# Dilated attention with a lent transposition bank and scores in two lots, in a two-block fp32 kernel with changed order in six other places

## Chip, cores and metric

The kernel runs on one core of one Trainium2 chip. The metric is the device time of the whole program in microseconds (us), lower is better. All matrix products are made from fp32 values that are split in two parts.

## What is computed

x is 256 tokens by 1024, mem and mem_2 are 256 by 1024. First an embedding norm and two layers with a hybrid mixer, attention to a memory, and a feed-forward net, each followed by a norm of the sum; then one layer of a second kind. Cut to what matters here:

```python
x = layer_norm(x)
for l in range(2):
    qa, ka, va, qb, kb, vb, gb, gc, hc, gates = split(x @ w_in[l])
    ya = rms_norm(diff_attention(qa, ka, va))          # 4 heads of two softmax maps (8 maps)
    yb = neighbourhood_attention(qb, kb, vb, rpb[l])   # 8 heads; scores + bias table, masked
    yc = gb * dwconv(gc * hc)                          # 512 channels, 3 taps
    h = sum(sigmoid(gate) * (y @ w_branch)) @ w_mix_out
    x = layer_norm(alpha * x + h)
    h = attention(x @ xa_q, mem @ xa_k, mem @ xa_v) @ xa_o    # 4 heads of 256
    x = layer_norm(alpha * x + h)
    x = layer_norm(alpha * x + conv_ffn(x))
y_mla = mla(rms_norm(x) @ w)                           # 8 heads, causal
y_dil = mixture of 3 groups x 4 heads of dilated attention, softmax over groups too
y_mem = 4 heads of attention to rms_norm(mem_2)
x = x + rms_norm((gated sum of three branches) @ w_o); x = x + rms_norm(conv_ffn(...))
```

## The kernel before

**Weights.** All weights come as one stream in the order of use: 525 halves of 512 KB, each four tiles of 256 columns. SyncE's queue loads them into five slots (RAW = 5; half h waits for the low part of half h - 5). ScalarE writes each half's high part (`weights_hi`, L1076) into one of four split slots (SPLIT = 4; it waits for the last use of half h - 4), VectorE subtracts for the low part (`weights_lo`, L1453). Both do this where `reach(key)` stands in their order: `AT` notes, while TensorE's program is written, at which half each step of TensorE stands, and `reach` splits all halves up to some ahead of that. TensorE waits for the low part of a half before its first tile (`half_at`).

**TensorE.** `linear` multiplies a block: per tile of 128 rows six matmuls (high x high, low x high, high x low, on two halves of 128) into one of four PSUM banks `general` (`ps`), taken in turn by `open_bank`, which waits until the bank's former content is read. Further PSUM: two score banks (`sc`), one for transposed probabilities (`tp`, the trace's probs_transposed; `bank=4` lends it), one for attention outputs (`po`). A transposition is a matmul with the identity (`transposes`, L656; `turn`, L733). Activations are kept as high and low parts too (`xT_hi`, `xT_lo`, `memT_hi`, `memT_lo`, `merged`, `memory_out`, `ffn_act`), in one large area in SBUF, of which the tables of position bias (`bias_tab`) also use a part.

**Attention.** Every set (da 8 maps, na 8 heads, xa 4, mla 8, dil 4, mem 4) is run in steps. At step s TensorE issues the scores of head s, the fillers of that step (blocks of projections that are wanted later), the values product of head s - 2 and the transpositions of head s - 1 (`turn`). In dil a head has three groups, hence three scores, three transposition sets and three copies. ScalarE per step: `exps` (L1119), evacuation of the fillers (L1087), the output of head s - 2, then `probs_out`, the copies of transposed probabilities out of `tp` (L1143). VectorE per step: `normed` of head s - 1 (L1627 to L1641), `maxima` of head s (bias added at L1607, maximum L1616, its negative L1621), then fillers, output and an extra piece of work, if there is one. For dil `exps` needs the negative maximum over all three groups.
Extra pieces of VectorE in da: `gated_conv` chunk 0 at step 4, mask for heads 0 to 3 at step 5 (`masked`, L1714), chunks 1 and 2 at step 6, mask for heads 4 to 7 at 7, chunk 3 at 8. Layer 0 and layer 1 use the same order.

**Beginning.** TensorE: idle work, 16 transpositions of memory, key blocks 0 and 1 of the memory, transpositions of the normed x, key blocks 2 and 3, layer 0. ScalarE: four copies of memT, split to half 4, norm, evacuations. VectorE: the low parts of memT, low parts of two halves, statistics of x, and so on. SyncE's queue: constants, memory, halves 0 and 1, x, halves 2 to 4, the constants' second part, and on.

**GpSimd.** It issues DMAs: rows and columns of parameters, two saves of the transposed memory to DRAM, 32 transfers that build the bias tables in DRAM (L2040, 16 for each layer), then, once the first x is normed and all these have landed, the transfer of a layer's tables into SBUF (L2048).

**Other places.** Behind cross attention four output blocks (`xo`); in layer 1 all eight transposition pairs of the second memory (`mem2T`) stand between blocks 1 and 2. Behind mla stand key block dk 4, the last values of mla, dk 5 and then dil; the last values of dil stand inside the first step of mem.

## Time and profile before

| | us |
|---|---|
| median of three timed runs | 1708.31 |
| lowest and highest | 1705.27, 1708.36 |
| profiled execution, its own time | 1707.84 |
| its span in the trace | 1705.7 |
| TensorE busy | 1647.5 (97%) |
| VectorE busy | 1159.2 (68%) |
| ScalarE busy | 875.8 (51%) |

The trace gives each instruction's start and length from the span's start. Layer 0 begins on TensorE at 48.0, layer 1 near 603, the last layer near 1150; the dilated set runs from about 1323 to 1412, the last feed-forward net from 1514. "[2.54 <-DVE ...]" behind an instruction is the time its engine stood idle ahead of it, and what ended that. The granted clock is a share of full speed, 2.4 GHz; 0.5 is 1.2 GHz.

### The profile page before, as it was taken

What the parts mean: (1) busy time and instruction counts of PE and PEld (TensorE: products, weight loads), DVE (VectorE), ACT (ScalarE), POOL (GpSimd) and SP (SyncE); (2) the same over time, 40 slices, a digit from 0 to 9 for tenths busy, and PEclk for the clock granted to TensorE, in tenths of its full rate; (3) what the DMA queues carried; (4) which work ended last, traced back from release to release, by engine and by line L of the source; (5) the groups of instructions that cost most, each with busy time, mean ns of one, the idle gap of its engine ahead of it and who ended that gap; (6) DMA issues with size and microseconds to landing.
All of it is one profiled execution on the core that took longest, in us unless ns stands there. A gap on an engine that the chain in (4) does not pass through costs nothing.

```text
span 1705.7 us, 32288 instructions
## 1 busy us (share of the span) xinstructions
PE 1647.5 (97%) x13694; PEld 1603.9 (94%) x13694; DVE 1159.2 (68%) x1718; ACT 875.8 (51%) x1317; POOL 39.2 (2%) x59
## 2 busy tenths in 40 slices
PE   7999999999999999999999999998999899999997
PEld 7998999989999999899998999998899789999997
DVE  5568778747666767877874866676566545867776
ACT  4444653545444554465355554446655445465555
POOL 3300000000000000000000000000000000000000
PEclk8999999999999999999999999999999999999999
DMA  9854466535555474446653556564535243545562
GB/s 327 244 194 144 139 208 237 196 112 198 192 179 203 158 248 151 145 140 209 235 216 104 181 180 208 180 199 137 198 124 187 100 163 134 183 151 186 185 209 89
DMA packets 82511, 305.90 MB, mean 179 GB/s; under 512 B 10657, under 2 KB 10785, under 8 KB 80193
## 3 DMA queue, kind: packets, MB, share of 16 engines
q1 hardware_dynamic: 76720, 279.44, 48.7%
q0 software_dynamic: 5648, 24.41, 4.7%
q8 instruction: 108, 1.77, 0.4%
q14 instruction: 35, 0.28, 0.1%
HBM read 300.59 MB, written 6.29 MB: 180 GB/s over the span
## 4 chain that ended last, share of the span: by engine, by line
PE 82%; DVE 12%; ACT 3%; issue 2%; DMA 1%; SPq 0%; DVEq 0%; ACTq 0%
PE general L596 52%; PE general L600 13%; PE scores L638 5%; DVE weights_lo L1453 3%; PE attention_out L638 2%; PE probs_transposed L638 2%; PE scores L714 2%; ACT weights_hi L1076 2%; PE attention_out L774 1%; PE probs_transposed L733 1%; DMA raw_weights<-in_stream 1%; ACT exp_ring L1119 1%; PE attention_out L816 1%; PE probs_transposed L600 1%; DVE softmax_stats L1616 1%
## 5 line engine op out<-in xcount | busy, mean ns | idle before, releaser
L1453 DVE TENSOR_TENSOR weights_lo<-raw_weights,weights_hi 128x1024 fp32r<-128x1024 f32 x525 | 632.7, 1222 | 421.4 <-ACT weights_hi L1076 419.9
L1076 ACT ACTIVATE weights_hi<-raw_weights 128x1024 fp32r<-128x1024 f32 x525 | 552.6, 1057 | 402.5 <-PE general L596 224.6
L596 PE MATMUL general<-xT_hi_part,weights_hi 128*128 128x256 f32 x2432 | 682.7, 281 | 4.4 <-DVE weights_lo L1453 1.9
L596 PE MATMUL general<-xT_lo_part,weights_hi 128*128 128x256 f32 x2432 | 675.0, 278 | 0.0
L596 PE MATMUL general<-xT_hi_part,weights_lo 128*128 128x256 f32 x2432 | 674.9, 278 | 0.0
L596 PEld LDWEIGHTS general<-xT_hi_part,weights_hi 128*128 128x128 f32 x2432 | 459.0, 189 | 12.6 <-issue 7.4
L596 PEld LDWEIGHTS general<-xT_lo_part,weights_hi 128*128 128x128 f32 x2432 | 457.9, 188 | 0.5
L596 PEld LDWEIGHTS general<-xT_hi_part,weights_lo 128*128 128x128 f32 x2432 | 457.7, 188 | 0.0
L1775 DVE SCALAR_TENSOR_TENSOR exp_ring<-general,param_cols,exp_ring 128x255 f32<-128x255 f32 (+1 forms) x176 | 76.8, 478 | 46.4 <-ACT exp_ring L1242 44.9
L1242 ACT ACTIVATE exp_ring<-general,param_cols 128x256 f32<-128x256 f32 x88 | 44.9, 561 | 69.8 <-PE general L596 69.8
L1119 ACT ACTIVATE exp_ring<-exp_ring,softmax_stats 128x256 f32<-128x256 f32 (+3 forms) x56 | 29.3, 525 | 96.9 <-DVE softmax_stats L1621 96.9
L600 PE MATMUL general<-weights_hi,xT_hi_part 128*128 128x256 f32 x272 | 77.7, 286 | 0.9 <-DVE xT_lo_part L1463 0.9
L600 PE MATMUL general<-weights_lo,xT_hi_part 128*128 128x256 f32 x272 | 76.2, 280 | 0.0
L600 PE MATMUL general<-weights_hi,xT_lo_part 128*128 128x256 f32 x272 | 76.2, 280 | 0.0
L638 PE MATMUL scores<-weights_hi,ffn_act_hi 128*128 128x256 f32 x264 | 74.1, 281 | 0.8 <-DVE weights_lo L1453 0.8
L638 PE MATMUL scores<-weights_lo,ffn_act_hi 128*128 128x256 f32 x264 | 74.2, 281 | 0.0
L638 PE MATMUL scores<-weights_hi,ffn_act_lo 128*128 128x256 f32 x264 | 74.1, 281 | 0.0
L1087 ACT ACTIVATE attention_area<-general 128x512 f32<-128x512 f32 x60 | 35.6, 593 | 57.1 <-PE general L596 36.9
L1119 ACT ACTIVATE exp_ring<-scores,softmax_stats 128x256 f32<-128x256 f32 x56 | 26.0, 470 | 66.2 <-DVE softmax_stats L1621 66.2
L600 PE MATMUL general<-weights_hi,merged_lo 128*128 128x256 f32 x192 | 54.0, 281 | 0.0
L600 PE MATMUL general<-weights_lo,merged_hi 128*128 128x256 f32 x192 | 54.0, 281 | 0.0
L600 PE MATMUL general<-weights_hi,merged_hi 128*128 128x256 f32 x192 | 53.9, 281 | 0.0
(293 smaller groups left out, 2994.1 us busy)
## 6 DMA issues: line engine op xcount, KB each, us to landing
raw_weights<-in_stream SPq DMA_DIRECT2D x525, 512.0 KB, 4.2
attention_area<-in_ln_rows POOLq DMA_DIRECT2D x9, 1024.0 KB, 5.0
bias_scratch<-in_rpb POOLq DMA_DIRECT2D x32, 96.0 KB, 14.4
attention_area<-bias_scratch POOLq DMA_DIRECT2D x2, 1536.0 KB, 7.8
memT_hi<-memT_scratch POOLq DMA_DIRECT2D x2, 1024.0 KB, 5.8
memT_lo<-memT_scratch POOLq DMA_DIRECT2D x2, 1024.0 KB, 9.1
attention_area<-in_mem SPq DMA_DIRECT2D x1, 1024.0 KB, 5.0
z_tok<-in_x SPq DMA_DIRECT2D x1, 1024.0 KB, 8.7
```

The lines of the kernel that those rows point to most:

```text
L596: ins = nc.tensor.matmul(ps[b][0:m, half * T:half * T + T], w[wk][:, half * m:half * m + m], x[xk_], start=first, stop=last, skip_group_ch ...
L600: ins = nc.tensor.matmul(ps[b][:, half * T:half * T + T], x[wk][:, half * P:half * P + P], w[xk_], start=first, stop=last, skip_group_chec ...
L638: ins = nc.tensor.matmul(down[2 * t + c][:, q * TILE_N:q * TILE_N + TILE_N], act[xk_][:, kc, t * P:t * P + P], w[wk][:, at:at + TILE_N], s ...
L714: ins = nc.tensor.matmul(dst[:, lo:hi], q, k, start=(c == 0), stop=(c == len(pairs) - 1))
L733: ins = nc.tensor.transpose(tp[:, kt * T + t * P:kt * T + t * P + P], e[:, kt * P:kt * P + P], ident)
L774: ins = nc.tensor.matmul(po[r0:r0 + m, c * T + lo:c * T + T], v, p[:, lo:T], start=first, stop=(g == parts - 1 and kt == 1))
L1076: nc.scalar.activation(hi_half(h), raw_half(h), ACT.Copy).then_inc(*hi_done.more())
L1087: nc.scalar.activation(dst, src[:, :].rearrange("p (c w) -> p c w", w=T), func, **kw).then_inc(*read(key))
L1119: ins = nc.scalar.activation(e, src, ACT.Exp, bias=st("nm", j, t, t + 1), scale=scale if from_psum else 1.0, accum_out=st("sum", j, t, t + 1))
L1242: ins = nc.scalar.activation(cbuf(i % 2, k)[:, c * T:c * T + T], src[:, c * T:c * T + T], ACT.Identity, bias=colp(b, ch, packed), scale=co ...
L1453: nc.vector.tensor_tensor(lo_half(h), raw_half(h), hi_half(h).bitcast(F32), ALU.subtract).then_inc(*lo_done.more())
L1775: ins = nc.vector.scalar_tensor_tensor(d, s, colp(w, 3 * ch + tap, packed), d, ALU.mult, ALU.add)
```

## The change

- Dilated set: the middle group's transpositions go to `ps[3]`, which `open_bank` leaves out as long as it is lent, so that two transposition sets can stand side by side (`turned`, `back`). Scores of groups 0 and 1 stay ahead of the fillers, those of group 2 go behind them; head 0's first two go ahead of block dk 5. The last values of dil go ahead of the memory scores.
- VectorE's extra pieces in da: mask for heads 0 and 1 at step 1, 2 to 5 at step 2, 6 and 7 at step 3; convolution chunks at steps 4, 5, 6 and 8.
- Beginning: the table of ScalarE is loaded ahead of the constants, the first half is split behind the first copy on both engines, three key blocks stand ahead of x's transpositions and the fourth behind them, in bank 4. The constants' second part is issued behind half 10. GpSimd's row and column transfers start with half 3's high part, its 32 bias transfers with half 11's, and the saves of memory come behind the first 16.
- Cross attention: block xq 1 ahead of the set, xq 2 before xv 2, in the stream too.
- Second memory: its transpositions in two lots, behind output blocks 1 and 2.
- Merged, memory output, feed-forward activations and rows move by 32 columns (SHIFT) in the area.

```diff
-        fa_hi, fa_lo = (sb(f"ffn_act_{k}", 4 * T, "area", c, F32R) for k, c in (("hi", 0), ("lo", 4 * T)))
-        mg_hi, mg_lo = (sb(f"merged_{k}", 8 * T, "area", c + 128, F32R) for k, c in (("hi", 8 * T), ("lo", 16 * T)))
-        xo_hi, xo_lo = (sb(f"memory_out_{k}", 8 * T, "area", c, F32R) for k, c in (("hi", 24 * T), ("lo", 32 * T)))
+        fa_hi, fa_lo = (sb(f"ffn_act_{k}", 4 * T, "area", c + SHIFT, F32R) for k, c in (("hi", 0), ("lo", 4 * T)))
+        mg_hi, mg_lo = (sb(f"merged_{k}", 8 * T, "area", c + 128 + SHIFT, F32R) for k, c in (("hi", 8 * T), ("lo", 16 * T)))
+        xo_hi, xo_lo = (sb(f"memory_out_{k}", 8 * T, "area", c + SHIFT, F32R) for k, c in (("hi", 24 * T), ("lo", 32 * T)))
...
-        xa_fillers = [[("xq", 1), ("xv", 2)], [("xq", 2)], [("xq", 3)], [("xv", 3)], [], []]
+        xa_fillers = [[("xq", 2)], [("xv", 2)], [("xq", 3)], [("xv", 3)], [], []]
...
+        def turned(name, g):
+            return ps[3] if name == "dil" and g == 1 else tp
...
+                    if state["lent"] and state["bank"] % 4 == 3:
+                        state["bank"] += 1
...
-                    if n > 0:
-                        pe.wait_ge(*pT_ready.at(n - 1))
+                    back = 1 if name != "dil" or g == 0 else 2 if g == 2 else 3
+                    if n >= back:
+                        pe.wait_ge(*pT_ready.at(n - back))
...
-                    if step < len(js) and name not in ("da", "na"):
+                    if step < len(js) and name == "dil":
+                        if step:
+                            scores(js[step], (0, 1))
+                    elif step < len(js) and name not in ("da", "na"):
                         scores(js[step])
...
                     for key in fillers[step]:
                         filler(key)
+                    if step < len(js) and name == "dil":
+                        scores(js[step], (2,))
...
             linear(("xk", 0), MT, DC, True, before=as_ready("memT"))
-            linear(("xk", 1), MT, DC, True)
+            for i in (1, 2):
+                linear(("xk", i), MT, DC, True)
...
             to_feature("xT0", z3)
-            for i in (2, 3):
-                linear(("xk", i), MT, DC, True)
+            linear(("xk", 3), MT, DC, True, bank=4)
...
+                filler(("xq", 1))
...
-                linear(("xo", 1), XO, DC, False)
-                if l == 1:
-                    for tile in (mem2_tile0, mem2_tile1):
-                        pe.wait_ge(*tile.at(0))
-                    to_feature("mem2T", mem2)
-                for cb in (2, 3):
+                for cb in range(1, 4):
                     linear(("xo", cb), XO, DC, False)
+                    if l == 1 and cb < 3:
+                        for tile in (mem2_tile0, mem2_tile1):
+                            pe.wait_ge(*tile.at(0))
+                        for i in (2 * cb - 2, 2 * cb - 1):
+                            transposes(("mem2T", i), mem2, 2 * i)
...
+            for key in blocks("dq", 0, 4) + blocks("dk", 0, 4):
+                pe.wait_ge(*when_read(key))
+            scores(set_jobs("dil")[0], (0, 1))
             filler(("dk", 5))
-            for key in blocks("dq", 0, 6) + blocks("dk", 0, 6):
+            for key in blocks("dq", 4, 6) + blocks("dk", 4, 6):
                 pe.wait_ge(*when_read(key))
+            if state["uses"][3]:
+                pe.wait_ge(*free[3].at(state["uses"][3] - 1))
+            state["lent"] = True
             held = attention("dil", dil_fillers)
...
-            held = attention("mem", mem_fillers, held=held)
+            held()
+            state["lent"] = False
+            held = attention("mem", mem_fillers)
...
-            act.wait_ge(*const_in.at(0))
+            act.wait_ge(*idle_work_set.at(0))
+            nc.scalar.activation(gain_tmp[:, 3, 0:1], blank[:, 0:1], ACT.Sqrt)
             for i in range(DC // 2):
...
                                      ACT.Copy).then_inc(*mem_hi.more())
+                if i == 0:
+                    split_to(1)
+            act.wait_ge(*const_in.at(0))
             split_to(SPLIT)
...
-                attention("da", da_fillers, {4: lambda: gated_conv((0,)), 5: lambda: masked(0),
-                                             6: lambda: gated_conv((1, 2)), 7: lambda: masked(4),
-                                             8: lambda: gated_conv((3,))})
+                attention("da", da_fillers, {1: lambda: masked(0, 2), 2: lambda: masked(2, 4), 3: lambda: masked(6, 2),
+                                             4: lambda: gated_conv((0,)), 5: lambda: gated_conv((1,)),
+                                             6: lambda: gated_conv((2,)), 8: lambda: gated_conv((3,))})
...
-            pool.wait_ge(*xin.at(0))
+            pool.wait_ge(*hi_done.at(SPLIT - 1))
             load_rows(0)
             pool.dma_start(col[:, :], a["cols"][0]).then_inc(*cols_in.more())
-            pool.wait_ge(*when_read(("memT", DC // 2 - 1)))
-            for k in range(2):
-                part, copy = mem_parts(k)
-                pool.dma_start(copy, part).then_inc(*mt_saved.more())
-            pool.wait_ge(*hi_done.at(SPLIT - 1))
+            pool.wait_ge(*hi_done.at(3 * SPLIT - 1))
...
+                if l == 0:
+                    pool.wait_ge(*when_read(("memT", DC // 2 - 1)))
+                    for k in range(2):
+                        part, copy = mem_parts(k)
+                        pool.dma_start(copy, part).then_inc(*mt_saved.more())
...
-            sp.dma_start(const[:, CONST_FIRST:CONST_N], a["const"][:, CONST_FIRST:CONST_N]).then_inc(*tables_in.more())
             for h in range(RAW, HALVES):
                 sp.wait_ge(*lo_done.at(h - RAW))
                 load_half(h)
+                if h == 2 * RAW:
+                    sp.dma_start(const[:, CONST_FIRST:CONST_N],
+                                 a["const"][:, CONST_FIRST:CONST_N]).then_inc(*tables_in.more())
```

## Rows read from the trace of the kernel before

**Rows 1.** The page: busy time of each engine; the chain that ended last.

```profile
PE 1647.5 (97%) x13694; PEld 1603.9 (94%) x13694; DVE 1159.2 (68%) x1718; ACT 875.8 (51%) x1317; POOL 39.2 (2%) x59
...
PE 82%; DVE 12%; ACT 3%; issue 2%; DMA 1%; SPq 0%; DVEq 0%; ACTq 0%
```

**Rows 2.** Waits of TensorE: what for, us in total, times, longest.

```profile
PE probs_transposed L733 <- ACT probsT_ring L1143: 6.2, 8, 1.7
PE probs_transposed L733 <- DVE exp_ring L1641: 5.1, 2, 2.5
PE scores L714 <- DVE exp_ring L1607: 3.9, 2, 2.6
```

**Rows 3.** Timeline of TensorE, beginning: start, us, what, [idle before].

```profile
6.34 1.94 PE L656 MATMUL general<-constants,attention_area 128*128 128x128 f32 x16 [0.15 <-DMA attention_area<-in_mem]
12.75 0.55 PE L596 MATMUL general<-memT_hi,weights_hi 128*128 128x256 f32 x1 [4.48 <-DVE weights_lo L1453]
...
34.75 0.58 PE L596 MATMUL general<-memT_hi,weights_hi 128*128 128x256 f32 x1 [4.68 <-DVE xT_lo_part L1463]
...
48.00 0.28 PE L596 MATMUL general<-xT_hi_part,weights_hi 128*128 128x256 f32 x1
```

**Rows 4.** Stretches: us, TensorE busy (instructions), granted clock, DMA share, GB/s.

```profile
12.50:19.50 7.00, 6.75 (x36) 0.58 1.04 417
34.50:48.00 13.50, 13.25 (x96) 0.84 0.97 245
164.00:172.00 8.00, 7.78 (x47) 0.79 0.51 157
246.00:280.00 34.00, 34.00 (x300) 1.00 0.59 194
280.00:303.00 23.00, 23.00 (x198) 1.00 0.77 288
```

**Rows 5.** Timeline of ScalarE and VectorE, beginning.

```profile
7.05 1.28 ACT L1261 ACT_TABLE_LOAD   x1 [7.05 <-PE general L656]
8.34 2.06 ACT L1261 ACTIVATE memT_hi<-general 128x512 fp32r<-128x512 f32 x4
...
12.64 1.06 ACT L1076 ACTIVATE weights_hi<-raw_weights 128x1024 fp32r<-128x1024 f32 x1 [0.35 <-DMA raw_weights<-in_stream]
...
11.38 2.36 DVE L1453 TENSOR_TENSOR weights_lo<-raw_weights,weights_hi 128x1024 fp32r<-128x1024 f32 x2
13.66 2.70 DVE L1482 BATCH_NORM_STATS2 norm_stats<-z_tok 128x6 f32<-128x256 f32 x8
```

**Rows 6.** Timeline of GpSimd, first 105 us.

```profile
54.46 12.26 POOL L2040 DMA_DIRECT2D bias_scratch<-in_rpb  x15 [26.75 <-issue]
82.04 1.65 POOL L2040 DMA_DIRECT2D bias_scratch<-in_rpb  x2 [15.32 <-issue]
90.92 0.60 POOL L2048 DMA_DIRECT2D attention_area<-bias_scratch  x1 [7.24 <-issue]
```

**Rows 7.** The page's DMA issues: KB each, us to landing.

```profile
attention_area<-bias_scratch POOLq DMA_DIRECT2D x2, 1536.0 KB, 7.8
```

**Rows 8.** Timeline of VectorE and TensorE, first attention set of layer 0.

```profile
117.18 0.88 DVE L1641 SCALAR_TENSOR_TENSOR exp_ring<-exp_ring,softmax_stats 128x256 f32<-128x256 f32 x2
...
142.23 1.75 DVE L1714 TENSOR_TENSOR attention_area<-attention_area,constants 128x1536 f32<-128x1536 f32 x1
...
121.92 0.60 PE L733 MATMUL probs_transposed<-constants,exp_ring 128*128 128x128 f32 x4
```

**Rows 9.** Timeline of TensorE: cross attention, layer 0; third output block, layer 1.

```profile
322.36 1.97 PE L714 MATMUL scores<-memory_keys,attention_area 128*128 128x256 f32 x8 [0.73 <-issue]
...
940.47 0.58 PE L600 MATMUL general<-weights_hi,memory_out_hi 128*128 128x256 f32 x1 [2.32 <-DVE memT_lo L1463]
```

**Rows 10.** Timeline of VectorE and ScalarE, dilated set, head 2.

```profile
1358.23 1.41 DVE L1616 TENSOR_REDUCE softmax_stats<-exp_ring 128x1 f32<-128x384 f32 x2
...
1360.49 0.92 ACT L1119 ACTIVATE exp_ring<-exp_ring,softmax_stats 128x768 f32<-128x768 f32 x1
```

More of the change, by code:

```diff
@@ L553, in _ @@
         def _(pe):
-            state = {"tile": 0, "bank": 0, "uses": [0] * 5}
+            state = {"tile": 0, "bank": 0, "uses": [0] * 5, "lent": False}
             def open_bank(key, b=None):
                 if b is None:
+                    if state["lent"] and state["bank"] % 4 == 3:
+                        state["bank"] += 1
                     b = state["bank"] % 4
@@ L680, in mark, with scores @@
                 AT[(stage.name, (event, j))] = state["tile"] // HALF_TILES
-            def scores(j):
+            def scores(j, parts=None):
                 name, i = job(j)
@@ L687, in scores @@
                     pe.wait_ge(*when_read(("xq", i)))
-                for g in range(parts_of(name)):
+                for g in parts or range(parts_of(name)):
+                    AT[(stage.name, ("scores", j, g))] = state["tile"] // HALF_TILES
                     n = number[(j, g)]
@@ L732, in turn @@
                         for kt in range(2 if spans(name)[t][1] - spans(name)[t][0] == 256 else 1):
-                            ins = nc.tensor.transpose(tp[:, kt * T + t * P:kt * T + t * P + P],
+                            ins = nc.tensor.transpose(turned(name, g)[:, kt * T + t * P:kt * T + t * P + P],
                                                       e[:, kt * P:kt * P + P], ident)
@@ L1140, in probs_out @@
                     if name in ("mla", "dil"):
-                        nc.scalar.activation(pT[:, slot * 512:slot * 512 + T], tp[:, 0:T], ACT.Copy)
-                        ins = nc.scalar.activation(pT[:, slot * 512 + 384:slot * 512 + 512], tp[:, 384:512], ACT.Copy)
+                        nc.scalar.activation(pT[:, slot * 512:slot * 512 + T], turned(name, g)[:, 0:T], ACT.Copy)
+                        ins = nc.scalar.activation(pT[:, slot * 512 + 384:slot * 512 + 512], turned(name, g)[:, 384:512],
+                                                   ACT.Copy)
                     else:
@@ L1262, in _ @@
                                      ACT.Copy).then_inc(*mem_hi.more())
+                if i == 0:
+                    split_to(1)
+            act.wait_ge(*const_in.at(0))
             split_to(SPLIT)
             layer_norm(0)
-            for i in range(2):
+            for i in range(3):
                 filler(("xk", i))
             gains("xT0", lambda c: cconst("emb_g", c), lambda c: cconst("emb_b", c))
-            for i in (2, 3):
-                filler(("xk", i))
+            filler(("xk", 3))
             for l in range(DEPTH):
@@ L1289, in _ @@
                 gains("ln0", lambda c: colp("ln_g", c), lambda c: colp("ln_b", c))
-                for key in (("xv", 1), ("xq", 0)):
+                for key in (("xv", 1), ("xq", 0), ("xq", 1)):
                     filler(key)
@@ L1463, in low, with gains @@
                 return nc.vector.tensor_tensor(dst, src, hi.bitcast(F32), ALU.subtract)
-            def gains(name, dst, between=None):
-                for i in range(DC // 2):
+            def gains(name, dst, between=None, pairs=range(DC // 2)):
+                for i in pairs:
                     reach((name, i))
@@ L1582, in maxima @@
                 number = NUM[stage.kind][0]
-                reach(("scores", j))
+                if name != "dil":
+                    reach(("scores", j))
                 if name in ("na", "mla", "dil"):
@@ L1586, in maxima @@
                 for g in range(parts_of(name)):
+                    if name == "dil":
+                        reach(("scores", j, g))
                     n = number[(j, g)]
@@ L1707, in gated_conv, with masked @@
                     low(YC[1][:, c, :], dst, YC[0][:, c, :]).then_inc(*yc_ready.more())
-            def masked(h):
+            def masked(h, n):
                 dve.wait_ge(*bias_in.at(0))
-                table = bias_tab[:, h:h + 4, :, :].rearrange("p h j k -> p (h j) k")
-                mask = const[:, CONST["na_mask"]:CONST["na_mask"] + 64].unsqueeze(1).to_broadcast([P, 4 * NJ, 64])
+                table = bias_tab[:, h:h + n, :, :].rearrange("p h j k -> p (h j) k")
+                mask = const[:, CONST["na_mask"]:CONST["na_mask"] + 64].unsqueeze(1).to_broadcast([P, n * NJ, 64])
                 nc.vector.tensor_tensor(table, table, mask, ALU.add).then_inc(*bias_ready.more())
@@ L1833, in _ @@
                     MT[0][:, 2 * i:2 * i + 2, :]).then_inc(*read(("memT", i)))
+                if i == 0:
+                    split_to(1)
             split_to(2)
```

15 lines of the change are left out of this document (8 added, 7 removed).

## Prediction, made before the changed kernel was run

> **What bounds the kernel now.** I read the page's busy row and its chain first: TensorE is busy 97% of the span and holds 82% of the chain, so only what keeps TensorE idle or slow is worth time [rows 1]. The list of its waits names the idle places: transpositions of probabilities that wait for ScalarE's copy (8 waits, up to 1.7 us), transpositions that wait for VectorE (2 of 2.5), and dilated scores that wait for VectorE's reading (2, the longer one 2.6) [rows 2]. Then the beginning in order of time: 4.48 us idle at 12.75 and 4.68 at 34.75 [rows 3], and the granted clock: 0.58 of full speed over the 7 us from 12.5, 0.84 over the 13.5 us from 34.5, 0.79 over the 8 us from 164, each behind an idle stretch of TensorE [rows 4]. That is the level of 1.2 GHz for part of the stretch; 0.79 of 8 us costs 1.7 us, 0.84 of 13.5 us costs 2.2, 0.58 of 7 us costs 2.9. My yardstick for a new long wait is 1.9 us of slow clock behind it.
>
> **Beginning.** Between 12.75 and 48.00 TensorE does 192 matmuls of the memory keys at 0.1133 us (300 in 34 us at full clock [rows 4]), 21.8 us, and 16 transpositions, 1.9 us [rows 3]: 23.7 of work in 35.25 us.
> Now: the 1.28 us table load that stands before the first copy (0.52, a quarter of 2.06) [rows 5] runs earlier, so that copy ends at 7.6 instead of 8.9. Between 6.3, when memory is in (the first transposition starts) and 12.64, when the third half is in, five pieces of 512 KB land (two halves, x as two, one half): 1.27 us each, so the first half is in at 7.5. Its high part, split right behind the first copy (1.06), ends at 8.7, its low part (half of 2.36) at 10.0 [rows 5]. TensorE starts at 10.05 instead of 12.75. VectorE has then the other low memory parts and the second half (13.0), statistics (2.70 [rows 5]) and two aggregations to 16.1, and the third half at 17.3; TensorE wants the second at 12.8 and the third at 15.7: 0.3 and 1.6 us of new waits. Three key blocks stand ahead of x's transpositions, and the fourth, in its own bank, behind them: it lasts 5.4 us, and covers the 4.68 us that the first gained columns took [rows 3]. So layer 0 starts at 10.05 + 23.7 + 1.9 = 35.7, against 48.00: **-12.3 us**. I count no slow clock here, since the longest idle stretches left are 1.8 and 1.6 us; a slow one would cost 1.7 to 2.9. The constants' second part, queued behind half 10 instead of half 4 on SP's queue, is issued near 24 and is wanted only behind the first six projections of layer 0: nothing.
> A rule beside it: the Trainium skill, ScalarE: Activation LUTs, What ACT_TABLE_LOAD costs, adds a drain of about 1.4 us to each load. Here the next copy begins 1.29 us after the load's start, so the trace shows no drain; by the page the beginning would give 1.4 us more.
>
> **Bias tables against the mask.** GpSimd's 32 table transfers now start when half 11's high part is done. That needs the last key block read: start of layer 0 plus 1.9. In the trace 15 of them are issued at 54.46 and the next two at 82.04 (27.6 us), the rows transfer that waits for all follows at 90.92 (8.9) and takes 7.8 to land [rows 6, 7]. With the order 15, then 1, the two saves of transposed memory (2 MB; 1.5 MB of tables take 7.8, so I take 8, bounds 5 and 10) and 13, then 3: 27.6 + 33.9 + 10.5 + 7.8 = 79.8, at best 74. The tables are in at layer start + 76 to 82. The first mask piece now stands at VectorE's step 1, where it arrives at 116.1 - 48.0 = 68.1 after the layer's start; it blocks everything behind it on VectorE: the norm of the second map (its last two steps take 117.18 to 118.06 [rows 8], three small ones ahead of them 1.1) and the low halves. TensorE wants that map at 121.92 [rows 8], start + 73.9. Mask piece (a quarter of 8 heads: 0.9, half of 1.75 [rows 8]) and norm end at start + 79 to 85. Stall 5 to 11 us, I take 8.5; plus 1.9 of slow clock and 1.0 for the 3.9 us of lead that VectorE has lost while it does the two other pieces: **+11.4**. In layer 1 the tables are there long before: nothing. These transfers and the saves no longer compete with the beginning's stream.
>
> **Spreading of mask and convolution.** In both layers the last pair's transposition waits for VectorE (2 waits, 5.1 us [rows 2]), which did two convolution chunks (5.1) in step 6 and half the mask (1.75) in step 7. Removed from that chain are 2.5 and 1.75, put ahead of step 5 are 0.8: the waits go, 5.1, with the slow clock of layer 0 (1.7), and about half of a 1.15 us wait behind it in layer 1: **-7.3**.
>
> **Cross attention.** The second query block covers the wait for the first one's reading, 0.73 us [rows 9], and the third no longer is fresh when wanted, which I put at 0.25: two layers, **-2.0**. **Second memory**: 2.32 us at 940.47 [rows 9], where the third output block wants the bank of a transposition; now a free bank is there; with 1.4 of slow clock **-3.7**.
>
> **Dilated set.** Here the order matters. Per head TensorE now issues two scores, the fillers, the third score, the values and transpositions of the head before. ScalarE's order is as before: exponentials of this head, then evacuation of the fillers, output, then the copies of the transposed probabilities. The exponentials need the maximum over all three scores. Let t be the end of the fillers. VectorE first owes the low part of the half whose slot the last filler frees: high part 1.06, low part 1.2: t + 2.6. Then bias, mask and add 0.9, maximum 1.41 [rows 10], 0.2: t + 5.2; exponentials 1.6 (0.92 for the two merged score blocks [rows 10], two thirds of it for the third): t + 6.85; two evacuations of 0.55 (a copy of that size took 0.52 [rows 5]); output 0.4; first copy 0.65: t + 8.6 for head 1, 9.0 to 9.3 for 2 and 3. TensorE has done the third score (0.7), the values (about 2, not at head 1) and the two sets of transpositions that two banks allow (six at 0.15 [rows 8], overlapping, 0.8) by t + 1.5 or t + 3.5. The third waits for the first's copy: 7.1, 5.5 and 5.8 us. Before, the exponentials ran under the fillers. Beside these a wait for the last key block of under 1 us stays (0.9), the second score of head 1 waits for VectorE's reading of head 0's third, 2.1, and 0.3 remains elsewhere: 21.7 us idle. Now it is 11.3: the 3.9 and the 6.2 of the waits [rows 2], the 0.9 and the 0.3. So +10.4, and three slow clocks of 1.9 against two of about 1.7: +2.2: **+12.6**. Lending the bank leaves three for the fillers, each free a step before its next use: nothing. Holding the last values ahead of the memory scores moves 2 us within a lead of 3: nothing.
>
> **Shifted tiles.** Branch matmuls run at 0.1133 us, merged ones at 0.1162 ([rows 4], 300 in 34 and 198 in 23 with their openings). Only the second kind's tile moves by 32 columns; but value projections from unmoved tiles are as slow, so I take 0; bounds: 2,200 such matmuls times 0.004, -9, to +1.
>
> **Sum.** -12.3 + 11.4 - 7.3 - 2.0 - 3.7 + 12.6 = -1.3. The profiled execution took 1707.84 (span 1705.7), 0.5 under the median of the three timed ones, 1708.31: **1706.5 us**.
>
> **Rivals.**
> 1. *Tables in time.* If transfers run faster without the start's traffic, or the queue takes more at once, all is in by start + 70 and the +11.4 is gone: 1695. For: the batches may not repeat; against: 26 us of the 27.6 lie under a stream as dense as layer 0's.
> 2. *The lent bank pays.* If ScalarE came to its copies before TensorE, the dilated waits would fall from 11.3 to about 2, with their slow clock: -11 for +12.6: 1683. Against: ScalarE's written order. That the stage doesn't do what it says is this rival turned round, and my forecast.
> 3. *Slower.* The slow clock holds longer: it decides if after each of the four new waits, all over 5 us, it costs the 2.9 of the first stretch instead of 1.9 (+4), if the beginning's two short waits bring it too (+2.9), and the tables are at their late end (+2.5): 1716.
> 4. *The shift speeds the moved tiles*: 1698.
>
> **How the numbers follow.** Forecast 0.54, its own range 1701 to 1712; rivals 0.15, 0.10, 0.14, 0.07. A measurement here can tell about 0.2%, 3.4 us. The forecast splits 0.16 faster, 0.27 same, 0.11 slower. Faster 0.16 + 0.15 + 0.10 + 0.07 = 0.48; same 0.27; slower 0.25. The range leaves out rival 2 and a tail: 1692 to 1716.
>
> **What would show it.** Beginning: first key matmul near 10, layer 0 near 35.7, full clock between. Mask: GpSimd's last two table batches late, one VectorE wait on the tables' transfer, a TensorE wait of 5 to 11 us near 110. Dilated: three waits of 5 to 7 us on ScalarE's copy, each with a slow clock behind. None at the third output block of layer 1. I'm wrong if the three dilated waits are under 2 us, or VectorE never waits for the tables.

## The result, and the profile after

The changed kernel took 1715.03 us (median of six, 1710.29 to 1718.97) against 1707.34 for the kernel before (median of six): ratio 1.0045, 95% interval 1.0033 to 1.0057. I had forecast 1706.5 with 0.25 for slower; the time lies 8.5 us above the forecast, inside the range, on the other side of no change. The profiled execution took 1710.29, the shortest of the six; a second profile of the same kernel, with a span of 1716.4, is used further down.

The page after, its busy row and its chain, answers to [rows 1]. TensorE's share of the chain fell from 82% to 76%, more of the end hangs on others.

```profile
PE 1641.9 (96%) x13694; PEld 1601.7 (94%) x13694; DVE 1159.7 (68%) x1720; ACT 872.8 (51%) x1317; POOL 39.2 (2%) x59
...
PE 76%; DVE 12%; ACT 3%; issue 3%; DMA 0%; ACTq 0%; DVEq 0%
```

The waits of TensorE after (what for: us in total, times, longest) answer to [rows 2]. The waits for ScalarE's copy grew from 6.2 us in 8 to 17.4 in 4, those for VectorE's norm in the first attention set from 5.1 to 10.3.

```profile
PE probs_transposed L741 <- ACT probsT_ring L1165: 17.4, 4, 6.7
PE probs_transposed L741 <- DVE exp_ring L1670: 10.3, 3, 8.4
```

*Beginning.* The timeline of TensorE (start, us, what, [idle before]) answers to [rows 3]: two short waits, and the third row is the first matmul of layer 0, at 35.70 instead of 48.00. The 4.68 us wait is gone.

```profile
10.28 0.36 PE L602 MATMUL general<-memT_hi,weights_hi 128*128 128x256 f32 x1 [1.70 <-DVE weights_lo L1479]
17.33 0.36 PE L602 MATMUL general<-memT_hi,weights_hi 128*128 128x256 f32 x1 [1.06 <-DVE weights_lo L1479]
...
35.70 0.28 PE L602 MATMUL general<-xT_hi_part,weights_hi 128*128 128x256 f32 x1
```

*Tables.* Timelines of GpSimd, VectorE and TensorE, layer 0, answer to [rows 6, 8]. The last table transfer is issued at 100.87, the rows transfer at 108.53; VectorE, done with its work at 103.85, waits 11.36 us for it, and TensorE 8.36 for VectorE.

```profile
100.87 0.83 POOL L2068 DMA_DIRECT2D bias_scratch<-in_rpb  x1 [19.66 <-DMA bias_scratch<-in_rpb]
108.53 0.60 POOL L2081 DMA_DIRECT2D attention_area<-bias_scratch  x1 [6.84 <-issue]
...
103.16 0.69 DVE L1685 TENSOR_TENSOR attention_area<-attention_area,general 128x512 f32<-128x512 f32 x1 [0.52 <-PE general L602]
115.21 0.96 DVE L1743 TENSOR_TENSOR attention_area<-attention_area,constants 128x768 f32<-128x768 f32 x1 [11.36 <-DMA attention_area<-bias_scratch]
...
118.14 1.12 PE L741 MATMUL probs_transposed<-constants,exp_ring 128*128 128x128 f32 x4 [8.36 <-DVE exp_ring L1670]
```

*Dilated set, head 1.* VectorE's maximum, ScalarE and TensorE. The maximum ends at 1342.4, ScalarE's exponentials run from 1342.65, then two evacuations, and only then the first copy at 1345.13; TensorE has stood since 1339.0. Heads 2 and 3 have the same picture.

```profile
1341.00 1.41 DVE L1645 TENSOR_REDUCE softmax_stats<-exp_ring 128x1 f32<-128x384 f32 x2
...
1342.65 0.61 ACT L1141 ACTIVATE exp_ring<-exp_ring,softmax_stats 128x384 f32<-128x384 f32 x1 [3.80 <-DVE softmax_stats L1650]
...
1344.18 1.06 ACT L1109 ACTIVATE attention_area<-general 128x512 f32<-128x512 f32 x2
1345.13 0.38 ACT L1164 ACTIVATE probsT_ring<-probs_transposed 128x256 f32<-128x256 f32 x1
...
1345.73 0.91 PE L741 MATMUL probs_transposed<-constants,exp_ring 128*128 128x128 f32 x3 [6.73 <-ACT probsT_ring L1165]
...
1368.84 0.90 PE L741 MATMUL probs_transposed<-constants,exp_ring 128*128 128x128 f32 x3 [5.04 <-ACT probsT_ring L1165]
...
1392.55 0.90 PE L741 MATMUL probs_transposed<-constants,exp_ring 128*128 128x128 f32 x3 [5.29 <-ACT probsT_ring L1165]
```

*Layer 1* is where I expected the spread mask and convolution to gain, with the tables long in. First the kernel before: the first row is an early matmul of the layer, the other two the waits at the last pair and at the first neighbourhood head.

```profile
610.06 0.36 PE L596 MATMUL general<-xT_hi_part,weights_hi 128*128 128x256 f32 x1 [1.60 <-DVE weights_lo L1453]
...
719.64 0.66 PE L733 MATMUL probs_transposed<-constants,exp_ring 128*128 128x128 f32 x4 [2.54 <-DVE exp_ring L1641]
729.23 0.65 PE L733 MATMUL probs_transposed<-constants,exp_ring 128*128 128x128 f32 x4 [1.15 <-DVE exp_ring L1646]
```

Then the changed one:

```profile
607.21 0.36 PE L602 MATMUL general<-xT_hi_part,weights_hi 128*128 128x256 f32 x1 [1.60 <-DVE weights_lo L1479]
...
696.24 1.14 PE L804 MATMUL scores<-attention_area 64*128 64x256 f32 x8 [1.32 <-ACT exp_ring L1141]
...
716.89 0.66 PE L741 MATMUL probs_transposed<-constants,exp_ring 128*128 128x128 f32 x4 [0.95 <-DVE exp_ring L1670]
726.47 0.66 PE L741 MATMUL probs_transposed<-constants,exp_ring 128*128 128x128 f32 x4 [1.15 <-DVE exp_ring L1675]
```

From the first row to the last it took 119.17 us before and takes 119.26 now. The 2.54 us wait became 0.95, the 1.15 stayed, and a wait of 1.32 appeared at the scores of the third pair, behind the pieces of mask that now stand at steps 2 and 3: 3.69 us of waits before, 3.42 after.

### The profile page after: what moved, and what is told of

It reads as the page before. It is cut to its first block, busy times and chain, and to the rows that moved or that the text cites. A ratio compares the mean times of both kernels' runs of the same rounds, so it can differ in the third digit from the quotient of the medians.

```text
span 1708.1 us, 32291 instructions
## 1 busy us (share of the span) xinstructions
PE 1641.9 (96%) x13694; PEld 1601.7 (94%) x13694; DVE 1159.7 (68%) x1720; ACT 872.8 (51%) x1317; POOL 39.2 (2%) x59
## 4 chain that ended last, share of the span: by engine, by line
PE 76%; DVE 12%; ACT 3%; issue 3%; DMA 0%; ACTq 0%; DVEq 0%
PE general L602 48%; PE general L606 12%; PE scores L644 5%; DVE weights_lo L1479 3%; PE attention_out L644 2%; PE probs_transposed L644 2%; PE scores L721 2%; ACT weights_hi L1098 2%; PE probs_transposed L741 1%; PE attention_out L782 1%; DVE softmax_stats L1645 1%; DVE x_tok L1537 1%; ACT exp_ring L1141 1%; DVE x_tok L1534 1%; PE attention_out L824 1%
## 5 line engine op out<-in xcount | busy, mean ns | idle before, releaser
L741 PE MATMUL probs_transposed<-constants,exp_ring 128*128 128x128 f32 x192 | 32.0, 288 | 29.9 <-ACT probsT_ring L1165 17.4
L741 PEld LDWEIGHTS probs_transposed<-constants,exp_ring 128*128 128x128 f32 x192 | 22.7, 146 | 35.7 <-ACT probsT_ring L1165 18.3
L606 PEld LDWEIGHTS general<-weights_hi,xT_hi_part 128*128 128x128 f32 x272 | 51.5, 189 | 2.5 <-issue 1.1
```

The source lines that it names most:

```text
L606: ins = nc.tensor.matmul(ps[b][:, half * T:half * T + T], x[wk][:, half * P:half * P + P], w[xk_], start=first, stop=last, skip_group_chec ...
L741: ins = nc.tensor.transpose(turned(name, g)[:, kt * T + t * P:kt * T + t * P + P], e[:, kt * P:kt * P + P], ident)
```

## The experiments

Each takes parts of the diff or adds one edit. Ratios are to runs of the kernel before that were timed beside them. A difference of 0.001 in ratio is 1.7 us; a difference between two of the kernels here is uncertain by 0.0015 to 0.0025, since both intervals enter it.

### The dilated set undone, the tables early, the shift alone, the mask late

**The changed kernel without the dilated change.** `turned`, `back`, the lent bank, the scores in two lots and the last values are as before.

> The changed kernel with the dilated set as before (scores of all groups ahead of the fillers, one transposition bank). Theory: the three waits of 5.0 to 6.7 us for ScalarE's copy and their slow clock are the dilated change's price; they vanish and the old short waits (11.3 us) return: the trace shrinks by 10 to 11 us against the changed kernel, so about 1700 profiled and 1704 timed, ratio to before 0.998. Rival: the timed executions of the changed kernel are some 5 us over its profiled one because its dilated waits sometimes cost more clock; then the timed gain is 14 to 16 us, ratio 0.995, and the spread of the runs shrinks to that of before (5 us).

Measured: 1705.09 us, ratio 0.9982 (0.9972 to 0.9991). The dilated change costs 0.0063, 10.8 us, the first theory; its uncertainty is some 2.6 us. The rival wanted 14 to 16. The spread of the twelve runs, 1700.48 to 1706.91, is about that of the kernel before.

**The changed kernel with GpSimd's transfers as before.**

```diff
-            pool.wait_ge(*hi_done.at(SPLIT - 1))
+            pool.wait_ge(*xin.at(0))
             load_rows(0)
...
-            pool.wait_ge(*hi_done.at(3 * SPLIT - 1))
+            pool.wait_ge(*when_read(("memT", DC // 2 - 1)))
+            for k in range(2):
+                part, copy = mem_parts(k)
+                pool.dma_start(copy, part).then_inc(*mt_saved.more())
+            pool.wait_ge(*hi_done.at(SPLIT - 1))
```

> The changed kernel with GpSimd's transfers in the order of before (saves of memory at once, bias transfers from half 3's high part on). Theory: the tables are in 22 us earlier, VectorE's mask at step 1 does not wait, the 8.4 us wait near 110 and its 3.9 us of slow clock go, and the beginning keeps its 12 us or gives back up to 3 of them to the returned traffic: 9 to 12 us under the changed kernel, ratio 0.998. Rival: the queue's batches take as long from any start, but the traffic in the beginning delays the stream, and layer 0 begins 5 us or more later than 35.7: gain 5 or less, ratio 1.001 or more.

Measured: 1708.74, ratio 1.0008 (0.9998 to 1.0018), 6.3 us under the changed kernel: between the two. Both halves of the question are in its trace, which is that of the longest of its twelve executions (1713.65). The waits for the tables are gone; but ScalarE gets its halves late in the beginning (start, us, what, [idle before]):

```profile
27.32 1.06 ACT L1098 ACTIVATE weights_hi<-raw_weights 128x1024 fp32r<-128x1024 f32 x1 [3.07 <-DMA raw_weights<-in_stream]
32.90 1.06 ACT L1098 ACTIVATE weights_hi<-raw_weights 128x1024 fp32r<-128x1024 f32 x1 [4.52 <-DMA raw_weights<-in_stream]
33.86 0.58 ACT L1109 ACTIVATE memory_keys<-general 128x512 f32<-128x512 f32 x1
...
34.49 1.12 PE L662 MATMUL general<-constants,z_tok 128*128 128x128 f32 x4 [3.91 <-ACT memory_keys L1109]
...
80.15 0.39 PE L602 MATMUL general<-xT_hi_part,weights_hi 128*128 128x256 f32 x1 [1.96 <-DVE exp_ring L1602]
```

The last row answers to one at 73.88 in the changed kernel: 6.3 us of the beginning are lost. So the later start of GpSimd's transfers is what gives a part of the beginning's gain, and what makes the tables late.

**The shift alone**, on the kernel before (the three lines with SHIFT in the diff, and the same for the rows).

> The kernel before with only the four tiles moved by 32 columns. Theory: no effect, ratio 1.000 (plus or minus 0.001), since value projections from unmoved tiles are as slow as merged ones. Rival: alignment matters, in one direction (matmuls from these tiles at 0.1133 us, 5 to 9 us faster, ratio 0.996) or the other (the 2 us that the feed-forward nets lost between the two traces, ratio 1.001).

Measured: 1707.85, ratio 1.000 (0.9991 to 1.0008). No effect, as forecast.

**The changed kernel with mask and convolution at the steps of before.**

> The changed kernel with VectorE's mask and convolution pieces at the steps of before. Theory: the wait for the tables (8.4 us and 3.9 of slow clock) and the waits of 1.2 and 1.3 us behind steps 2 and 3 go, the two waits of 2.5 us at the last pair return with 1.7 of slow clock in layer 0: 9 us under the changed kernel, ratio 0.999. Rival: the tables are also late for step 5 and part of the wait remains there: under 5 us of gain.

Measured: 1704.01, ratio 0.9978 (0.997 to 0.9987): the early mask costs 0.0067, 11.4 us, more than the 9 expected. In the trace the wait for the tables is gone and the last pair waits 2.39 us in layer 0 and 2.54 in layer 1 (2.54 and 2.54 before).

### What adds up, and what each half of a part is worth

**Dilated set, mask and convolution undone together.**

> The changed kernel with both the dilated set and VectorE's mask and convolution pieces as before: what is left is the beginning, GpSimd's order, cross attention, second memory and the shifted tiles. Theory: the two undone parts cost 10.4 us (from the kernel without the dilated change) and 11.6 (from the one with the late mask), they add up, and the rest brings 14 us: 1693.5, ratio 0.9916. My prediction's terms for the rest (-12.3, -2.0, -3.7) would give 18 us: ratio 0.9895. Rival: the costs overlap (a clock that is slow for one stall is slow for the next) and the rest brings under 10: ratio 0.994 or more.

Measured: 1693.34, ratio 0.9917 (0.9903 to 0.9931), the first theory: what remains brings 14.2 us, and 10.8 + 11.4 - 14.2 = 8.0 against the 7.7 us that the change cost.

It also settles the spreading in layer 0. From the row at 74.08 that answers to the 73.88 of the changed kernel, to the first matmul of cross attention's second query block (309.01) this kernel, with the mask late, takes 234.9 us. The kernel with early tables and early mask takes 234.9 for the same (80.15 to 315.04). With the tables in time the new places are worth nothing, good or bad. The two profiles of the changed kernel take 246.3 and 247.9 us for this stretch, so the late tables alone cost 11.4 and 13.0.

Layer 1, where the tables are in for every kernel, says the same in more executions. Between the same two places it takes 234.87 to 235.08 us in five executions with the pieces spread, and 234.82 to 235.08 in four with them late. Even the slow clock makes no difference to this stretch: behind the last pair's wait in layer 0 the granted clock is 0.79 of 8 us here and 1.00 in the changed kernel with the mask late, and the stretch takes 234.9 and 235.1. With the slow clock the wait of 1.26 us at the first neighbourhood head (162.50 in the other kernel) is missing: TensorE comes to it later and finds VectorE ready.

**The lent bank**, added to that kernel; scores of all three groups ahead of the fillers. The expectation says that the last values stay where they were; in the kernel that ran they go ahead of the memory scores, as in the changed kernel.

```diff
+            return ps[3] if name == "dil" and g == 1 else tp
...
+                    back = 1 if name != "dil" or g == 0 else 2 if g == 2 else 3
+                    if n >= back:
+                        pe.wait_ge(*pT_ready.at(n - back))
...
+            state["lent"] = True
             held = attention("dil", dil_fillers)
```

> The same with the lent bank added to the dilated set, but the scores of all three groups ahead of the fillers and the last values where they were. Theory: the second bank is good by itself, and the order of the scores is what costs: most of the eight waits for ScalarE's copy (6.2 us) go, some 4 us and 1 to 2 of slow clock, ratio 0.003 under the kernel without it. Rival: with three banks for the fillers the open banks become late and take it back, ratio equal.

Measured: 1685.17, ratio 0.9871 (0.9858 to 0.9884), 0.0046 or 7.9 us better, uncertain by some 3. The bank is good: of the seven waits of 0.64 us three of 0.32 are left, and the first, 1.75 before, is 1.42. No wait of a filler for a bank appears. In the profiled executions the stage is 5.2 us shorter (the table further down). The moved last values have no part in it: from the transpositions of the last group (1389.91, now 1383.93) to those of the last feed-forward net (1493.97, now 1488.00) it is 104.1 us both times.

```profile
1335.58 0.55 PE L740 MATMUL probs_transposed<-constants,exp_ring 128*128 128x128 f32 x3 [1.42 <-ACT probsT_ring L1156]
...
1352.66 0.55 PE L740 MATMUL probs_transposed<-constants,exp_ring 128*128 128x128 f32 x3 [0.32 <-ACT probsT_ring L1156]
```

**The beginning alone**, on the kernel before, with GpSimd's and SyncE's orders.

> The kernel before with only the reordered beginning and the order of GpSimd's and SyncE's transfers; VectorE's mask stays at steps 5 and 7. Theory: layer 0 begins 12.3 us earlier and nothing gives it back, because step 5 comes later than the tables: ratio 0.9928. Rival: part of the gain is lost behind, since the transfers that left the beginning now run beside layer 0's stream: ratio 0.995.

Measured: 1697.67, ratio 0.9939 (0.9925 to 0.9952): 10.4 us, interval 8.2 to 12.8. It stands between the two theories and decides neither. In its trace 11.6 us are there at the wait near 86 (86.19 before, 74.55 now) and 8.2 at the last wait (1692.00 before, 1683.77 now). About 3 us go in layer 1. Of these 1.9 go behind the wait at the last pair: it passed at full clock before (1.00 of 8 us), and here the granted clock behind it is 0.60. Another 1.05 go between the first wait of the layer (599.39) and 631.99, at full clock and without a wait; why is open. 2 us return near 940, where the clock is 0.81 of 8 us in the kernel before and 1.00 in this one.

**ScalarE's copies ahead of the exponentials**, in the changed kernel.

```diff
                 for step in range(len(js) + 2):
-                    if step < len(js):
+                    if step < len(js) and name != "dil":
                         exps(js[step])
...
                     if 1 <= step <= len(js):
                         probs_out(js[step - 1])
+                    if step < len(js) and name == "dil":
+                        exps(js[step])
```

> The changed kernel, with ScalarE's exponentials of the dilated set moved behind the fillers' evacuation, the output and the copies of the transposed probabilities. Theory: the waits of 6.7, 5.0 and 5.3 us come only from the exponentials standing ahead of the copies (they need the maximum over the third score, which now comes last); with the copies first they fall under 1 us each, their slow clock goes with them, and nothing else is late, since the exponentials are wanted a step later: 20 us under the changed kernel, 1695, ratio 0.993. Rival: late exponentials delay VectorE's norm and the next transpositions, and half of the gain is lost: ratio 0.998.

Measured: 1694.46, ratio 0.9927 (0.9915 to 0.994), 0.0118 or 20 us under the changed kernel. It is the reason for the three waits, shown: the copy now stands ahead of the exponentials (start, us, what, [idle before]), and the wait of 6.73 is 0.76.

```profile
1344.08 0.37 ACT L1164 ACTIVATE probsT_ring<-probs_transposed 128x256 f32<-128x256 f32 x1
...
1347.98 0.62 ACT L1141 ACTIVATE exp_ring<-exp_ring,softmax_stats 128x384 f32<-128x384 f32 x1 [2.17 <-DVE softmax_stats L1652]
...
1344.67 0.55 PE L741 MATMUL probs_transposed<-constants,exp_ring 128*128 128x128 f32 x3 [0.76 <-ACT probsT_ring L1165]
```

### The better orders together, and where the mask's work can go

**One convolution chunk moved from step 6 to step 8**, on the kernel with the lent bank only.

```diff
-                                             6: lambda: gated_conv((1, 2)), 7: lambda: masked(4),
-                                             8: lambda: gated_conv((3,))})
+                                             6: lambda: gated_conv((1,)), 7: lambda: masked(4),
+                                             8: lambda: gated_conv((2, 3))})
```

> The kernel with the lent bank only (1685.2, ratio 0.9871), with one of the two convolution chunks of step 6 moved to step 8, behind the last pair. Theory: a piece of VectorE's work moved within the attention set moves the wait and does not remove it: the waits of 2.4 us at the last pair shrink, that at the first neighbourhood heads (1.2 to 1.3) grows by as much; ratio within 0.001 of 0.9871. Rival, the step of my prediction: the waits of 2.4 us and one slow clock go and nothing comes back, 5 to 7 us, ratio 0.984 or less.

Measured: 1688.47, ratio 0.9885 (0.9868 to 0.9901). Nothing is gained. It is 0.0014 worse, a little outside what I gave, but the two intervals overlap. In layer 1 the wait at the last pair (2.39) is gone and that at the first neighbourhood head grew from 1.34 to 3.41. First without the move, then with it:

```profile
706.06 0.66 PE L740 MATMUL probs_transposed<-constants,exp_ring 128*128 128x128 f32 x4 [2.39 <-DVE exp_ring L1658]
715.64 0.66 PE L740 MATMUL probs_transposed<-constants,exp_ring 128*128 128x128 f32 x4 [1.34 <-DVE exp_ring L1663]
```

```profile
705.67 1.13 PE L803 MATMUL scores<-attention_area 64*128 64x256 f32 x8 [0.34 <-ACT attention_area L1100]
716.81 0.66 PE L740 MATMUL probs_transposed<-constants,exp_ring 128*128 128x128 f32 x4 [3.41 <-DVE exp_ring L1663]
```

2.39 + 1.34 = 3.73 against 0.34 + 3.41 = 3.75: the wait moved. In layer 0 the longer wait (3.35) was followed by a granted clock of 0.79 of 8 us, and the stretch up to the second query block takes 236.6 us instead of 235.1; in layer 1 it passed at 1.00, and the stretch is 234.8.

**The changed kernel with the mask late and the copies first.**

> The changed kernel with two of its orders put right: mask and convolution at the steps of before, and in the dilated set ScalarE's copies ahead of the exponentials. Theory: gains add up as before, 1694.5 less 11.4 (what the wait for the tables cost) is 1683, ratio 0.986. It also tells whether scores in two lots are worth having: in the traces the last layer takes 331 us with them and the copies first, 336 with the lent bank alone, so it should be 2 to 5 us under the kernel with the lent bank only. Rival: the two are equal, 1685.

Measured: 1680.99, ratio 0.9846 (0.9827 to 0.9864), 26 us under the kernel before and 35 under the changed one (1716.06 when timed beside it); this is the version that beats both. It is 0.0025 or 4.3 us under the kernel with the lent bank only, with intervals that just overlap. The traces separate the two better. The stage that holds the dilated set, from the first projection behind the gates of the last layer (1228.22 in the changed kernel) to the transpositions of the last feed-forward net (1513.04) takes, in all the profiled executions:

| dilated set | us | executions |
|---|---|---|
| order of before | 273.1 to 275.6 | 5 |
| changed kernel's order | 284.8 to 288.5 | 4 |
| lent bank, all scores early | 268.3 and 269.6 | 2 |
| lent bank, scores in two lots, copies first | 264.4 to 264.8 | 3 |

So two lots with the copies first beat all scores early by some 4 us. Whether the scores or the copies bring these 4 us is not shown: the order with the copies first and all scores early was not run.

**The same with the chunk at step 8.**

> The same with one convolution chunk moved from step 6 to 8. Theory: as above, no gain from the move, ratio within 0.001 of the kernel without it. Rival: 5 to 7 us less.

Measured: 1685.74, ratio 0.9876 (0.986 to 0.9891), 0.003 worse, and neither theory. In its trace the first neighbourhood heads wait 3.5 and 3.4 us where the last pair had waited 2.5 and 2.5. The stretches to the second query block take 236.5 and 237.7 us, against 234.9 and 234.8 in the kernel without the move. That is 4.5 us of the 5; besides, memory came 1 us later in this execution. The granted clock behind the long waits is 0.79 or 0.80 of 8 us in both kernels, which loses 1.7 us each time. In the kernel without the move nothing comes of it: at full clock another wait of 1.3 us for VectorE follows (near 715 in the kernel with the lent bank only), and this one is gone. Behind the moved wait there is none that could take the loss up, so the 1.7 stay in each layer. The other 1.2 us, in layer 1, are lost at full clock and without a wait; why is open.

**The changed kernel again.**

> The changed kernel itself, to have it beside the others on one chip and a second profile of it. Theory: 1.0045 again, and where this profiled execution is longer than the first (1710.3), the longer part shows as more clock at 1.2 GHz behind the four long waits (2.4 to 3.9 us behind each) and a longer wait for the tables, not as new waits. Rival: it is at 1710, as the first profile, and the sum of the parts (10.4, 11.6 and -14) is 2 to 5 us off.

Measured: 1716.06, ratio 1.0048 (1.0034 to 1.0062). Its profiled execution took 1718.53, 8.2 more than the first one, with the same waits but one: that for the tables is 9.90 instead of 8.36. The windows of TensorE (us, busy (instructions), granted clock, DMA share, GB/s) show what happened at the long waits. First profile:

```profile
112.00:128.00 16.00, 9.72 (x58) 0.68 0.32 122
1324.00:1340.00 16.00, 13.54 (x110) 1.00 0.40 142
1340.00:1356.00 16.00, 10.27 (x70) 0.79 0.13 39
```

Second profile, the same places:

```profile
112.00:128.00 16.00, 8.63 (x53) 0.68 0.38 139
1328.00:1344.00 16.00, 14.59 (x107) 0.89 0.34 110
1344.00:1360.00 16.00, 9.26 (x54) 0.68 0.18 62
```

Behind the same wait of 2.02 us (near 1325 and 1329) the clock stayed at 1.00 the first time and fell to 0.89 of 16 us the second. Around the first long dilated wait it was 0.79, then 0.68. Taken over the 8 us behind each wait of 6.7, 5.0 and 5.3 us it was 0.79, 0.74 and 0.72, then 0.65, 0.66 and 0.67.

Of the 8.2 us, 1.5 are there behind the wait for the tables and 3.3 came in the dilated set, between 1316.45 and 1408.97 of the first profile. The other 3.4 lie elsewhere, among them 1.1 behind the wait of 3.56 at the start of the last layer, where the clock was 1.00 of 8 us in the first profile (near 1151) and 0.63 in the second (near 1153). The theory holds for a little more than half.

## Why the prediction was wrong

By its own steps, forecast and measured, in us:

| Step | forecast | measured | from |
|---|---|---|---|
| beginning | -12.3 | -10.4 (-12.8 to -8.2) | that part alone |
| bias tables against the mask, and spreading of mask and convolution | +11.4 - 7.3 = +4.1 | +11.4 | mask and convolution undone |
| cross attention, second memory, shift | -5.7 | -3.8 | 0.9917 less 0.9939 |
| dilated set | +12.6 | +10.8 | that part undone |
| sum | -1.3 | +8.0 | the change itself: +7.7 |

The last three parts are differences of two measurements and uncertain by 2.5 to 3.3 us each.

**The step that failed is the spreading.** I wrote that from the last pair's chain 2.5 and 1.75 us are removed and 0.8 put ahead, so "the waits go, 5.1", and with clock and a following wait 7.3. That counts only the pair that work leaves. The wait at the last pair fell only to 0.95 us; behind the pieces at steps 2 and 3 stand waits of 1.17 (layer 0) and 1.32 (layer 1) at the scores of the third pair; that at the first neighbourhood head stayed. In layer 1 the stretch is 119.17 and 119.26 us, in layer 0, with tables in time, 234.9 and 234.9. I priced it at -7.3 and it is 0. The 1.7 of slow clock in that sum was worth nothing either, since the stretch is as long with it as without. This alone turns the forecast's sign: -1.3 + 7.3 = +6.0. That VectorE's lateness is carried from pair to pair and sets the length of the set fits the placements tried, but for the chunk at step 8, where slow clock came on top. It was not measured by itself, for instance with the pieces left out.

**Right, mechanism and size.** The beginning: first key matmul forecast for 10.05, was at 10.28; layer 0 for 35.7, was at 35.70, without a slow clock. That it is right to the hundredth is luck: the waits inside it were one of 1.06 us and not 1.9 in two, and the late start and small gaps made up the rest. The tables: I put their landing at the layer's start plus 79.8, which is 115.5; VectorE's first mask piece begins at 115.21. TensorE's wait was forecast at 8.5 and measured at 8.36 and 9.90. The dilated set: waits of 7.1, 5.5 and 5.8 us forecast, 6.73, 5.04 and 5.29 found, for the reason given, which the kernel with the copies first shows.

**Right as far as the runs can tell.** Of the beginning's 12.3 us timed runs kept 10.4, with an interval that holds 12.3. Cross attention and second memory brought 3.8 of 5.7, uncertain by some 3 us; their waits did go in the trace (0.73 us twice, 2.32 once), and nothing shows that a term of theirs was off. The dilated set cost 10.8 for 12.6, uncertain by 2.6; in the traces of the stage, 287.1 against 274.4 us in the mean, it is 12.7.

**Rivals.** The slower one, 1716, gave the right time partly by luck. Two of its three conditions hold in part. It put 2.9 us of slow clock behind each long wait for my 1.9, and the four waits over 5 us cost 2.8, 1.7, 2.1 and 2.2 in the first profile and 2.6, 2.8, 2.7 and 2.6 in the second (what the granted clock of the 8 us behind each lacks). So my yardstick was low, by 1 to 3 us in all. It put the tables at their late end: they were in at the layer's start plus 79.5 in the first profile and plus 81.0 in the second, of 76 to 82. The third did not hold, since the beginning's short waits brought no slow clock. It kept the spreading at -7.3, and the loss of that is larger than what it had right. Rival 2 fell as forecast: the bank did not pay, because of ScalarE's order. I had named that order as what stands against it and had not thought of turning it round. Tables in time fell too, and making them so gave 6.3 of 11.4 back, since it disturbs the beginning.

## What to carry to other kernels

Where one engine is late through a whole set, moving its side work moves the wait; price the places that it moves to like the one that it leaves, and take only what the whole stretch gains. Slow clock costs nothing while the late engine still sets the pace, and its full price behind the last wait for it. An extra buffer pays only if the engine that empties it comes to it in its own written order: here the bank, with scores in two lots, cost 10.8 us with the exponentials ahead of the copies, and with the copies first the stage became the shortest of all. A transfer that is delayed to clear one stage needs its consumer's place checked in the next: the mask at step 1 and the tables' later start were each harmless without the other.

## What the hardware showed

The slow clock behind a wait is partly chance in this kernel. The 2.54 us wait of layer 1 near 720 was followed by full clock in the kernel before; the wait at the same place (2.37 us, near 710) in the kernel with only the beginning changed was followed by a granted clock of 0.60 of 8 us. That loses 3.2 us; 1.9 of them stayed, since the next wait (1.15 before) was gone. The 2.02 us wait in the dilated set passed at 1.00 and at 0.89. The granted clock is at its lower level, 1.2 GHz, behind every wait of 5 us or more (0.64 to 0.79 of the 8 us behind it, in all the traces), and returns only once TensorE has worked again: around the 8.36 us wait for the tables it is 0.50 from 114 on, where TensorE had stood since 109.8, and back at 1.00 from 124 on, with TensorE at work since 118.14. The Trainium skill, TensorE: Matmul & The Clock Gate, Part 1: The HAM clock gate (What's actually happening), says that "the default state is throttled, and activity releases the throttle". The traces agree. This chance is enough for 5 to 8 us between two executions of the changed kernel (1710.29 and 1718.53), and one profile is not a price.

The table load of ScalarE ran at 0.73 us for 1.28, and the next activation began at 2.03, 1.30 after its start. The drain of 1.4 us that the Trainium skill, ScalarE: Activation LUTs, What ACT_TABLE_LOAD costs, adds to a load is not seen in this trace either. Nor is it at a load between two activations: at 732.07 one starts 0.02 us behind an activation's end, and the next activation begins at 733.36, 1.29 after the load's start. The rows of the first load:

```profile
0.73 1.28 ACT L1281 ACT_TABLE_LOAD   x1 [0.73 <-PEq L2314]
2.03 0.20 ACT L1281 ACTIVATE probsT_ring<-probsT_ring 128x1 f32<-128x1 f32 x1
```
